# First attention of a two-block transformer kernel: value products of two units put together behind the second unit's transposes, with a third SBUF home for transposed maps

## The reference

```python
s_s = einsum('bghqd,bgqnkd->bghqnk', qc, k_sel) * scale      # selected blocks
p_s = _masked_softmax(s_s, mask_s)
o_s = einsum('bghqnk,bgqnkd->bghqd', p_s, v_sel)
...
s_w = einsum('bghqd,bgkd->bghqk', qc, kw) * scale            # window
p_w = _masked_softmax(s_w, mask_w)
o_w = einsum('bghqk,bgkd->bghqd', p_w, vw)
return gc[..., 0:1] * o_c + gc[..., 1:2] * o_s + gc[..., 2:3] * o_w
```

## The kernel before

| unit | query tile, branch | keys per head | scores (PE) | transposes (PE) | values (PE) | copy (ACT) |
|---|---|---|---|---|---|---|
| j0 | 0, BOTH | 2 x 128 | 4 of 128x128 | 4 | 4 | 128x512 |
| j1 | 3, 0 | 512 | 2 of 128x512 | 8 | 8 | 128x1024 |
| j2 | 1, BOTH | 2 x 256 | 4 of 128x256 | 8 | 8 | 128x1024 |
| j3 | 3, 1 | 512 | 2 of 128x512 | 8 | 8 | 128x1024 |
| j4 | 2, 0 | 384 | 2 of 128x384 | 6 | 6 | 128x768 |
| j5 | 2, 1 | 384 | 2 of 128x384 | 6 | 6 | 128x768 |

## Time and profile before

### The profile page before, as it was taken

The page is one execution under the profiler, slowest core; times in us unless marked ns, Lnnn a source line. Parts: engine busy times, 40 slices in busy tenths (PEclk is TensorE's granted clock), DMA queues, the critical chain, the costliest instruction groups (busy, mean ns, idle before and its releaser), DMA issues.

```text
span 1722.0 us, 22517 instructions
## 1 busy us (share of the span) xinstructions
PE 1686.9 (98%) x8985; PEld 1338.6 (78%) x8985; DVE 1027.0 (60%) x1667; ACT 645.1 (37%) x1017; POOL 60.6 (4%) x84
## 2 busy tenths in 40 slices
PE   7999999999999999999999999999999999999899
PEld 6888888787866678768888888888888866677687
DVE  5665444456887756347444457643554587878674
ACT  4222222241257742333222233312222567556830
POOL 0000000000012210000000000000000000002200
PEclk9999999999999999999999999999999999999999
DMA  6655433246300015313333233324332333402322
GB/s 204 207 163 176 133 98 90 74 125 195 94 1 2 2 53 146 96 49 81 104 94 97 89 105 98 91 84 121 89 96 81 101 104 98 132 10 62 92 80 73
DMA packets 235372, 167.61 MB, mean 97 GB/s; under 512 B 10437, under 2 KB 221629, under 8 KB 235141
## 3 DMA queue, kind: packets, MB, share of 16 engines
q1 hardware_dynamic: 232948, 161.98, 32.4%
q10 hardware_dynamic: 2320, 4.20, 0.7%
HBM read 156.31 MB, written 6.30 MB: 94 GB/s over the span
## 4 chain that ended last, share of the span: by engine, by line
PE 87%; DVE 8%; ACT 2%; issue 1%; SPq 1%; DMA 1%; POOL 0%; DVEq 0%; ACTq 0%
PE bank L1070 24%; PE bank L1072 24%; PE bank L1071 24%; PE turned L1319 3%; PE bank L1307 2%; PE bank L1345 2%; PE bank L1492 1%; PE bank L1409 1%; DVE w_lo L1722 1%; DVE Pm L2420 1%; DVE bank L2113 1%; PE bank L1618 1%; PE turned L1398 1%; ACT Pm L1016 1%; PE turned L1128 1%
## 5 line engine op out<-in xcount | busy, mean ns | idle before, releaser
L1070 PE MATMUL bank<-h_hi,w_hi 128*128 128x512 f32 x1200 | 472.6, 394 | 3.0 <-DVE h_lo L1777 1.5
L1071 PE MATMUL bank<-h_lo,w_hi 128*128 128x512 f32 x1200 | 467.3, 389 | 0.0
L1072 PE MATMUL bank<-h_hi,w_lo 128*128 128x512 f32 x1200 | 467.2, 389 | 0.0
L649 ACT ACTIVATE w_hi<-w_raw 128x2048 fp32r<-128x2048 f32 (+3 forms) x134 | 236.8, 1767 | 490.6 <-PE bank L1072 490.0
L1722 DVE TENSOR_TENSOR w_lo<-w_raw,w_hi 128x2048 fp32r<-128x2048 f32 (+3 forms) x133 | 280.0, 2106 | 55.3 <-ACT w_hi L649 52.6
L1070 PEld LDWEIGHTS bank<-h_hi,w_hi 128*128 128x128 f32 x1200 | 225.2, 188 | 60.2 <-issue 11.6
L1072 PEld LDWEIGHTS bank<-h_hi,w_lo 128*128 128x128 f32 x1200 | 225.3, 188 | 47.3
L1071 PEld LDWEIGHTS bank<-h_lo,w_hi 128*128 128x128 f32 x1200 | 225.3, 188 | 46.6 <-issue 0.7
L1070 PE MATMUL bank<-u_hi,w_hi 128*128 128x512 f32 x352 | 137.1, 389 | 0.0
L1071 PE MATMUL bank<-u_lo,w_hi 128*128 128x512 f32 x352 | 137.0, 389 | 0.0
L1072 PE MATMUL bank<-u_hi,w_lo 128*128 128x512 f32 x352 | 136.9, 389 | 0.0
(11 more groups left out here) (425 smaller groups left out, 2359.9 us busy)
## 6 DMA issues: line engine op xcount, KB each, us to landing
w_raw<-in_w_in SPq DMA_DIRECT2D x28, 1024.0 KB, 5.5
w_raw<-in_ffn_w_gate SPq DMA_DIRECT2D x44, 512.0 KB, 4.0
w_raw<-in_ffn_w_up SPq DMA_DIRECT2D x44, 512.0 KB, 5.3
w_raw<-in_ffn_w_down SPq DMA_DIRECT2D x32, 704.0 KB, 4.6
ada_w<-in_ada_w SPq DMA_DIRECT2D x16, 768.0 KB, 6.6
w_raw<-in_w_in SPq DMA_DIRECT2D x19, 512.0 KB, 4.2
w_raw<-in_w_out SPq DMA_DIRECT2D x8, 1024.0 KB, 5.0
w_raw<-in_w_branch_nsa SPq DMA_DIRECT2D x8, 512.0 KB, 5.5
```

Of the source, the lines that this page charges most:

```text
L649: act.activation(w_hi[s % 2][:, 0:n], w_raw[s % 2][:, 0:n], ACT.Copy).then_inc(s_hi, 1)
L1070: pe.matmul(o, l[0], r[0], start=first, stop=False)
L1071: pe.matmul(o, l[0], r[1], start=False, stop=False)
L1072: return pe.matmul(o, l[1], r[0], start=False, stop=last)
```

## The change

PE's loop keeps scores(u + 2) and turn(u) in each step, and values(u - 1) up to and with u = 20 (`PAIRED`). From u = 21 on an odd step has no values, and an even step has values(u - 2) and values(u - 1), both behind turn(u). The values of units 54 and 55 stand behind the loop. Since the values of a unit come up to a step later, transposed maps get a third home, `PTm2`, in 4 KB that nothing else uses at that time; the units from 20 on go round the three homes, and evac(u) waits from unit 22 on for the values of u - 3 in place of u - 2. The second attention keeps its two homes.

```diff
+        PTm.append(at("PTm2", [P, 2, S], F32, N0 + 34 * KB))
...
+        PAIRED = UNITS.index((2, 0, BOTH))
+        assert PAIRED % 2 == 0 and (U0 - PAIRED) % 2 == 0
+        turned_home = lambda u: (u - PAIRED) % 3 if PAIRED <= u < U0 else u % 2
+        home_left_by = lambda u: u - 3 if PAIRED + 2 <= u < U0 else U0 - 1 if u in (U0, U0 + 1) else u - 2
...
             def evac(u, n, maps):
                 act.wait_ge(sem("pt_full"), u + 1)
                 if u >= 2:
-                    act.wait_ge(sem("pv_done"), attended(u - 2))
-                act.activation(PTm[u % 2][:, 0:maps, 0:n], turned[:, 0:maps, 0:n], ACT.Copy).then_inc(sem("pt_evac"), 1)
+                    act.wait_ge(sem("pv_done"), attended(home_left_by(u)))
+                act.activation(PTm[turned_home(u)][:, 0:maps, 0:n], turned[:, 0:maps, 0:n], ACT.Copy).then_inc(sem("pt_evac"), 1)
...
-                                ins = pe.matmul(place(e, t), vtok[:, b, c:c + 64], PTm[u % 2][:, e, k * P:(k + 1) * P],
+                                ins = pe.matmul(place(e, t), vtok[:, b, c:c + 64], PTm[turned_home(u)][:, e, k * P:(k + 1) * P],
...
                 if u + 2 < U0:
                     scores(u + 2)
                 turn1(u)
-                if u:
+                if 0 < u <= PAIRED:
+                    values(u - 1)
+                elif u > PAIRED and u % 2 == 0:
+                    values(u - 2)
                     values(u - 1)
...
+            values(U0 - 2)
             values(U0 - 1)
```

## The result

| | before | changed |
|---|---|---|
| median device time, 9 runs each | 1723.58 us (1722.68 to 1725.27) | 1728.43 us (1727.9 to 1729.82) |
| ratio to before, 95% interval | | 1.0026 (1.0018 to 1.0034) |
| profiled execution, its own time | 1723.94 us | 1728.24 us |
| its span | 1722.0 us | 1726.3 us |
| unit 22's transposes to the first `rqk` matmul | 95.51 us | 100.14 us |

The change makes the kernel slower by 0.26%, with an interval of 3.1 to 5.9 us; the medians differ by 4.85 us. The forecast was 1727.6, +4.0. All ratios in this document compare fast executions alone; one of the seven of e2 took 5931 us and is left out of its ratio.

A forecast was written before the change was run, and what follows sets the result against it. PE, busy 98% of the span, was taken as the bound; 3.6 us from units 22 to 54 plus 0.5 at the end gave +4.1, rounded to 4.0, on the median 1723.58: 1727.6 us, range 1725.2 to 1729.8.

The forecast's parts named there:

- The bound: First attention: PE, busy 16.93 of 16.93 us in a head pair, sets the time by its own order of work.
- The saving: On PE, two groups of values side by side save one change of array shape, 0.16 us per pair of units.
- the rule: A change of tiling mode drains the engine; by that alone 17 even steps save 17 x 0.16 = 2.7 us.
- The wait for the copy: Transposes behind an odd unit wait for ACT's copy of `turned`: 2.28 us between transposes, 1.85 for six transposes.
- the half-hidden rival: Copy's semaphore precedes its recorded end, or shape change falls inside the wait: +0.7 to +2.2 us, 1725.8; chance 0.22.
- POOL: An even unit's transposes also wait for POOL's weighting: 2.24 us from j1 to j2, 1.97 from j5 to j0.
- One head pair: Six steps of the new order, transposes to transposes, take 17.57 us against 16.93, +0.64.
- Start and end: Unit 22 to unit 54: 93.45 us against 89.86, +3.6; from there to the projection: 6.14 against 5.65, +0.5.
- The third home: The copy now waits for the values of u - 3, ahead of transposes it needs anyway; costed at nothing.
- The sum: Attention and its end together: 3.6 + 0.5 = +4.1 us, rounded to 4.0 since the copies' gap rests on one row.
- the third rival: POOL and DVE run late in short steps, weighting ends after the copy, 0.4 us more a pair: 1729.6; chance 0.12.
- the first two rivals: Copy wait hidden, saving whole: 2.7 us gained, 1720.9, chance 0.08; copy wait half hidden: 1725.8, chance 0.22.

The follow-up runs named there:

- e2: The changed order of values with the two old homes for transposed maps instead of three; ratio to the kernel before 1.0027, head pair 17.59 us.
- e4: Kernel before plus third home, with only the values behind j4's transposes held back, without unit 54; ratio to before 0.9996, head pair 16.78 us.
- e1: Kernel before with the third home and the copy's new wait, old order of values; ratio to before 0.9997, head pair 16.93 us.
- e9: Changed kernel with the copies of odd units 21 to 53 cut to each map's first 128 columns; ratio to before 1.0005, head pair 17.01 us.
- e7: Changed kernel with the copy split into two instructions from unit 20, first map's transposes waiting for the first only; ratio to before 1.0019, head pair 17.25 us.
- e11: The changed kernel itself run again beside the kernel before; ratio to before 1.0024, head pair 17.59 us, attention 102.30 us.
- e12: Repeat of the kernel that, against the one before, holds back only the values behind j4's transposes; ratio to before 1.0002, attention 97.34 us.
- e10: Against the kernel before: third home, values held at j4 in head pairs 2 to 5, values a step later from unit 48; ratio 1.0001, attention 96.95 us.
- e13: Repeat of the version held at j4 in head pairs 2 to 5 with values later from unit 48; ratio to before 0.9998, attention 96.96 us.
- e3: Kernel before plus third home, with only the values behind j3's transposes held back; ratio to before 1.0017, head pair 17.38 us.

## Why the prediction was right

**The bound.** That PE's own order sets the time held: in the steady head pair PE is idle now only where transposes wait, and the attention's loss appears in the span (+4.3 us against +4.65 for the attention from unit 21 on).

**The saving.** 0.16 us for each pair of groups put together: e4 shows 0.15, with nothing else changed but the third home, which e1 shows to cost nothing. It hangs on the shape and not on the group: behind the last values of a head pair the compressed branch reads other operands in the same shape, and no second 0.16 is paid there (576.84 to 578.52 in the earlier trace rows, 28 records in 1.68). The Trainium skill says ("TensorEngine Tiling (Array Packing)", Key Properties) that a change of tiling mode drains TensorE; the trace agrees, with 0.15 to 0.16 us for each change that is spared. Taken alone the rule forecast a gain, and the kernel lost; it was right to price it as a term and not as the result.

**The wait for the copy.** 2.28 worked out, 2.30 measured behind both j1 and j3. It rested on one row for the gap between copy and transposes (0.15, taken as 0.12), and that gap is there again: the copy behind j3 starts 1.13 behind its transposes and ends at 571.19 (570.16 + 1.03), and the next transposes start at 571.33 in the rows, 0.14 later. The 0.02 us between 2.28 and 2.30 is the 0.03 that the prediction took off this gap. The kernel before had the same distance once, at its end, from the transposes of unit 53 to those of unit 54 (618.80 to 621.10, 2.30). e9 takes most of the copy away and the wait goes with it; e7 halves the copy and the step behind j3 falls by 0.43.

The row of unit 53's transposes in the kernel before (that of unit 54's is in the earlier trace rows):

```profile
618.80 1.09 PE L1319 MATMUL turned<-cst,Pm 128*128 128x128 f32 x8
```

ACT's rows for the copy behind j3 in the changed kernel:

```profile
570.16 1.03 ACT L832 ACTIVATE PTm<-turned 128x1024 f32<-128x1024 f32 x1 [1.18 <-PE turned L1324]
571.08 0.57 ACT L823 ACTIVATE Pm<-bank,mstat 128x384 f32<-128x384 f32 x1
```

ACT goes on 0.1 before the copy's recorded end, and the half-hidden rival built on that. It fell: PE does not go on before the recorded end but 0.14 behind it.

**POOL.** 2.24 and 1.97 worked out; 2.26 (e7, e9) and 1.98 to 1.99 measured. In the changed kernel it decides at j0, and at j2 only in the two head pairs of the first profile in which its weighting took longer.

**One head pair.** 17.57 worked out, 17.59 to 17.60 measured. The six steps were 3.98, 2.28, 3.32, 2.28, 3.74, 1.97 and came out as 3.98, 2.30, 3.30, 2.30, 3.73, 1.99.

**Start and end.** Unit 22 to unit 54: 93.45 worked out, 94.01 in the first profile and 93.56 in e11. From there to `rqk`: 6.14 worked out, 6.13 measured in both. That the first `rqk` matmul came at 630.64, for 630.8 forecast, is luck in part: unit 22's transposes began 0.74 us earlier than before (530.50 for 531.24), and the stretch behind them was 0.5 us longer than worked out.

**The third home.** Nothing expected, nothing found in the steady part (e1, e2); two homes cost 0.2 us at the end of the loop (e2).

**The sum.** From unit 22's transposes on, +4.1 worked out, +4.63 in the first profile, +4.18 in e11 (93.56 + 6.13 against 95.51). The difference between the two is mostly two head pairs in which j1 to j2 took 2.46. The sign of the third rival is there (POOL alone named, a step over 2.4), but not its mechanism: POOL didn't begin late, it began 1.00 us behind j1's transposes as in the other pairs (581.03 to 582.03), and its instructions took 0.20 us longer. The prediction had no term for that. It came in two of the pairs of one execution and not in the other. What the prediction took off, "round 4.0 since the copies' gap rests on one row", was not called for. The chance of 0.59 for "slower" was held down by the first two rivals, which no run bears out (0.05 and 0.22), and by 0.11 of the forecast itself, which stood close to the limit of 0.2%.

## What to carry to other kernels

Where one engine is busy without a gap, an order that saves it set-up time has to be laid out step by step against the round trip of every buffer it waits for: here from transposes to transposes 2.30 us through one PSUM home, against 1.67 to 1.87 us of PE's own work once the values had been moved out. A third SBUF home is no help when the home that is reused fastest is another one. And the same edit can be a gain or a loss by where it falls: look for the steps at which the remaining work is as long as the round trip, as at j4, and change only these. Here that took 0.8 us off the attention, which no comparison of whole executions shows.

## What the runs showed of the hardware

**POOL and DVE trade time.** While POOL weights the first map of j2, DVE weights the second. Mostly POOL's two instructions took 1.20 us in all and DVE's 0.94. In two head pairs of the first profile it was this:

```profile
582.03 1.40 POOL L596 TENSOR_SCALAR Pm<-Pm,mstat,gates 128x256 f32<-128x256 f32 x2 [2.84 <-DVE mstat L2147]
...
582.44 0.74 DVE L2161 TENSOR_SCALAR Pm<-Pm,mstat,gates 128x256 f32<-128x256 f32 x2
...
583.49 0.55 PE L1324 MATMUL turned<-cst,Pm 128*128 128x128 f32 x3 [0.53 <-POOL Pm L596]
```

What DVE gained, 0.20, POOL lost, and PE's step took 2.46 for 2.30. It was in no pair of the other thirteen profiles. Why it comes in some pairs stays open.

**The attention repeats, the rest scatters.** The same attention took 98.11 us in two kernels (before, e1), 97.34 in e4 and e12, and 96.95 and 96.96 in e10 and e13. The exception is the changed kernel, 102.76 and 102.30, by the two head pairs above. The span less the attention was anything from 1622.5 us (e7) to 1625.9 (e3), though this part is the same code in all of them but for its place. So an edit of 1 us shows in the timeline of one profile and not in the medians of some ten runs. In e7 the medians even lie 1.9 us above what its attention says (+4.1 against +2.2). Its interval of 1.6 to 4.8 us holds both, and its profiled execution, 1725.25 us, was the shortest of its ten.
